# Sixteen gate tiles of a merge move into the state-space stage, and the order of dense steps and attention units changes

## The chip, the cores and the metric

The kernel runs on one core of a Trainium2 chip. A core has a matmul engine (TensorE), a vector engine (VectorE), an activation engine (ScalarE), a general one (GpSimd), and SyncE, which issues the DMAs here. The metric is the device time of one execution in microseconds. The kernel before takes 5170.65 us, the median of three runs (5169.60 to 5171.93).

## The reference

Everything is float32, with one sequence of 512 tokens (and 256 context tokens), model width 1024. A first block has two branches on a common projection `hl @ w_in`: RWKV, a recurrence over 16 heads, and a state-space model (SSM) over 4 groups of 8 heads with 128 states, chunk by chunk, in both directions, on the tokens in column-major order of a grid of 64 columns. The two are merged by gates, then come a router and 16 experts. The second block stands twice (two layers): dilated attention, latent attention and stick-breaking attention, three gated branches, and a feed-forward part. What the change touches:

```python
def merge(ya, yb, gates, p):
    ga, gb = jnp.split(jax.nn.sigmoid(gates.astype(F32)), 2, axis=-1)
    ya = jnp.einsum('blc,cd->bld', ya, p['proj_a'])
    yb = jnp.einsum('blc,cd->bld', yb, p['proj_b'])
    return jnp.einsum('bld,de->ble', ga * ya + gb * yb, p['w_out']).astype(gates.dtype)

# one chunk of the SSM (ssd_chunked), and stick-breaking attention of one block of 128 queries
y_intra = jnp.einsum('bijg,bijge,bjgep->bigep', cb, seg, xdt)
y_inter = jnp.einsum('bign,bgepn->bigep', c_c, h) * jnp.exp(cum)[..., None]
log_one_minus = jnp.where(strict, jax.nn.log_sigmoid(-z), 0.0)
after = lax.cumsum(log_one_minus, axis=3, reverse=True) - log_one_minus
weights = jnp.exp(jnp.where(strict, log_beta + after, -jnp.inf))
```

## The kernel before

The program has stages: start, RWKV, SSM, merge, experts, and twice the second block. Each stage has one function per engine (`ssm_sync`, `ssm_tensor`, `ssm_vector`, `ssm_scalar`, `ssm_gpsimd`, and so on), and between stages the engines meet: each waits until the other three have come (`meet`). Inside a stage a function yields the order of all steps, and each engine walks through this one order and issues its own share of every step, waiting on semaphores. TensorE thus works strictly in that order.

**SSM** (`ssm_order`, L1499). `turns` takes one step each from a list of generators in rotation: the decays, the forward scan, the projector, the backward scan, the projector again, the reader. So a turn has two projector steps. The projector makes, for each of four groups, six tiles `("conv", g, ci, s)` in seven steps (steps 0 to 3 hold two matmuls each of the projection, step 2 also the transposes of the tile before, steps 4 to 6 nothing for TensorE) and four tiles `("z", g, i, s)` of the gate z in two steps of four matmuls. A scanner has for each of six chunks `values`, `carry`, and for the four last ones also `masks`, `weights`, `apply`. `apply` multiplies the weights of the chunk with the values, eight heads of 64 columns in a bank of PSUM. The reader gates and squares the result (`read` 0 to 3) and transposes and stores it to DRAM (`ybd`, `read` 4 to 7). A group's projection starts when the read of the group two before is done (L1513), a group's scan when its z is done. The projections read `b.hp`, the input in column-major order; at the end of the stage `hp` is copied back to `k.hL` in row order, three engines at once, and the normalizer is brought to row order in `k.rb`.

**Merge** (`merge_tensor`, L2013). For each of eight tiles d of 128 output columns and each branch: eight matmuls with `hL` for the gate, then 8 (`proj_a`, on `yaT`) or 16 (`proj_b`, on `ybT`) for the branch. `yaT` (2 MB) and `ybT` (4 MB) are read from DRAM. SyncE loads weights into a ring of six areas, in the order `wg`, `pa`, `pb`.

**Second block** (`block2_order`, L2430). Attention units (head pair, block of 128 queries) run on six lanes. `drain` takes one step from each lane in rotation and mixes in dense steps (two matmuls of 512 columns, or four steps to a tile) of a second generator: each attention step adds n to `due`, and each whole unit of `due` takes one dense step. The stretches are: before meeting A (first projections and rotations), `softA` (dilated attention, with the latent projections), `softB` (latent attention), `stick` (stick-breaking) up to meeting C. The dense steps are the 24 gate tiles (`("gate", d, br, s)`, d from 0 to 7), `chan` and `tok`. A unit with row block i has 128(i + 1) keys, and in `Unit` (L2546) the units of `stick` take i = 0, 1, 2, 3 by pairs.

The helper lines that the rows name are L224 (a matmul), L227 (a transpose), L235 to L259 (VectorE), L282 (ScalarE), L337 (a load of a ring) and L470 (another load).

## Time and profile before

| | |
|---|---|
| median of three runs | 5170.65 us |
| profiled execution, own time | 5169.21 us |
| its span | 5167.4 us |
| TensorE busy | 4649.1 us (90%), 35892 instructions |
| VectorE, ScalarE, GpSimd busy | 2123.6, 1300.3, 435.4 us |
| mean clock of TensorE | 0.944 of full |
| DMA | 494.88 MB, mean 96 GB/s |

The span is from the first to the last instruction. A busy time counts an engine's instructions on that stretch; a matmul instruction of the program in float32 stands in the trace as two records. "Idle before" is the time in which an engine had nothing to do just ahead of the instruction, with what released it.

### The profile page before, as it was taken

Reading aid. Unit: us, or ns where it says so; the run is one execution under the profiler, and the core shown is the slowest. Engines: PE = TensorE matmul, PEld = TensorE weight load, DVE = VectorE, ACT = ScalarE, POOL = GpSimd, SP = SyncE. Lnnn points to the kernel's source line nnn. Section 1 sums busy time; section 2 is a strip of 40 time slices with the busy share of each in tenths; the row PEclk is TensorE's granted clock in tenths of the full one; section 3 lists DMA queues with packets and bytes.
Section 4 is the critical chain, followed back from the end, with each engine's and each line's share of the span. In section 5 each row is a group of like instructions: output and inputs, shape, how many; then the busy total and the mean of one; then the engine's idle time right before and its main releaser. Section 6 shows DMA issues by size and latency. Waiting matters only on the chain.

```text
span 5167.4 us, 84303 instructions
## 1 busy us (share of the span) xinstructions
PE 4649.1 (90%) x35892; PEld 2888.0 (56%) x35892; DVE 2123.6 (41%) x3933; ACT 1300.3 (25%) x2411; POOL 435.4 (8%) x387
## 2 busy tenths in 40 slices
PE   6899889988988969979999898979999998979999
PEld 3566666676554544465343554534777554544777
DVE  3555555553354461021111346473343346473333
ACT  2343333342222310010000123232232123241222
POOL 0121111110231330000000000020000000020000
PEclk8999999998989989989999899999999999989999
DMA  5200000001101004227999221113321221113221
GB/s 224 78 18 18 18 9 14 5 5 45 43 33 41 25 17 187 83 85 317 399 406 374 95 74 65 41 41 128 114 82 49 86 76 62 43 58 134 91 98 49
DMA packets 72783, 494.88 MB, mean 96 GB/s; under 512 B 9032, under 2 KB 9560, under 8 KB 29784
## 3 DMA queue, kind: packets, MB, share of 16 engines
q1 hardware_dynamic: 72408, 489.49, 24.5%
q8 instruction: 283, 4.64, 0.4%
q14 instruction: 92, 0.75, 0.0%
HBM read 468.47 MB, written 21.00 MB: 95 GB/s over the span
## 4 chain that ended last, share of the span: by engine, by line
PE 72%; issue 9%; DVE 9%; PEld 3%; DMA 3%; ACT 2%; POOL 1%; SPq 0%; PEldq 0%; POOLq 0%; DVEq 0%; ACTq 0%
PE ps L224 69%; PEld ps L224 3%; PE ps L227 3%; DMA upper<-in_ew 2%; DVE upper L235 2%; ACT upper L282 1%; DVE upper L243 1%; DVE upper L259 1%; POOL upper L3350 1%; DVE lower L235 1%; DVE upper L251 1%; DVE lower L243 1%; ACT lower L282 0%; DVE upper L239 0%; DVE lower L239 0%
## 5 line engine op out<-in xcount | busy, mean ns | idle before, releaser
L224 PE MATMUL ps<-lower 128*128 128x512 f32 (+9 forms) x6512 | 1967.3, 466 | 81.8 <-issue 25.1
L224 PEld LDWEIGHTS ps<-lower 128*128 128x128 f32 (+3 forms) x6512 | 997.4, 197 | 787.6 <-issue 609.4
L224 PE MATMUL ps<-upper 64*64 64x64 f32 (+7 forms) x15552 | 827.5, 258 | 125.4 <-DVE upper L251 44.0
L282 ACT ACTIVATE upper<-ps 128x512 f32<-128x512 f32 (+6 forms) x963 | 435.8, 483 | 1860.1 <-PE ps L224 1342.5
L224 PEld LDWEIGHTS ps<-upper 64*64 64x64 f32 (+4 forms) x15552 | 597.7, 145 | 437.2 <-issue 231.8
L224 PE MATMUL ps<-lower,upper 64*64 64x64 f32 (+6 forms) x7536 | 723.8, 315 | 55.2 <-DMA lower<-in_ada 20.8
L224 PE MATMUL ps<-rounded 128*128 128x512 f32 x3072 | 720.0, 397 | 30.6 <-DVE rounded L235 23.1
L224 PEld LDWEIGHTS ps<-rounded 128*128 128x128 f32 x3072 | 583.9, 190 | 165.9 <-ACT rounded L282 26.3
L224 PEld LDWEIGHTS ps<-lower,upper 64*64 64x64 f32 (+3 forms) x7536 | 383.0, 144 | 338.5 <-issue 279.7
L282 ACT ACTIVATE upper<-upper 128x768 f32<-128x768 f32 (+11 forms) x619 | 326.9, 534 | 735.8 <-DVE upper L255 205.8
L224 PE MATMUL ps<-upper,lower 128*128 128x512 f32 (+5 forms) x1584 | 483.0, 474 | 9.0 <-DVE lower L243 2.7
L259 DVE COPY_PREDICATED upper<-lower,ps 128x256 f32<-128x256 uint8 (+2 forms) x576 | 246.4, 457 | 326.5 <-PE ps L224 290.9
L224 PEld LDWEIGHTS ps<-upper,lower 128*128 128x128 f32 (+1 forms) x1584 | 249.3, 199 | 228.9 <-issue 211.4
L251 DVE COPY upper<-ps 128x64 f32<-128x64 f32 (+8 forms) x423 | 166.9, 405 | 449.6 <-PE ps L224 406.5
L227 PE MATMUL ps<-lower,upper 128*128 128x128 f32 (+1 forms) x1204 | 191.8, 294 | 132.0 <-ACT upper L282 61.4
L235 DVE TENSOR_TENSOR rounded<-lower,rounded 128x512 fp32r<-128x512 f32 (+2 forms) x136 | 200.9, 1477 | 257.4 <-ACT rounded L282 257.2
L235 DVE TENSOR_TENSOR upper<-upper,ps 128x512 f32<-128x512 f32 (+1 forms) x136 | 108.5, 798 | 481.6 <-PE ps L224 472.4
L282 ACT ACTIVATE rounded<-lower 128x512 fp32r<-128x512 f32 (+2 forms) x136 | 171.7, 1263 | 405.3 <-PE ps L224 270.3
L227 PEld LDWEIGHTS ps<-lower,upper 128*128 128x128 f32 (+1 forms) x1204 | 145.9, 148 | 223.2 <-issue 115.7
L282 ACT ACTIVATE lower<-ps 128x512 f32<-128x512 f32 (+1 forms) x178 | 104.5, 591 | 446.5 <-PE ps L224 416.7
L243 DVE SCALAR_TENSOR_TENSOR upper<-ps,lower,upper 128x511 f32<-128x511 f32 (+1 forms) x208 | 130.1, 625 | 141.0 <-ACT upper L282 135.1
L3337 POOL COPY upper<-lower 128x512 f32<-128x512 f32 x8 | 4.9, 613 | 2048.2 <-PE ps L224 2047.4
(81 smaller groups left out, 2193.2 us busy)
## 6 DMA issues: line engine op xcount, KB each, us to landing
lower<-in_ew SPq DMA_DIRECT2D x144, 1024.0 KB, 10.4
upper<-in_ew SPq DMA_DIRECT2D x48, 1024.0 KB, 13.5
lower<-in_b0f SPq DMA_DIRECT2D x16, 2048.0 KB, 7.8
lower<-in_b1f SPq DMA_DIRECT2D x16, 2048.0 KB, 7.7
upper<-in_ada SPq DMA_DIRECT2D x18, 1024.0 KB, 5.6
lower<-in_wrkv SPq DMA_DIRECT2D x8, 1728.0 KB, 7.6
lower<-in_b0g SPq DMA_DIRECT2D x8, 1536.0 KB, 6.4
gad<-upper SPq DMA_DIRECT2D x48, 256.0 KB, 2.0
```

Source lines behind the costliest of these rows:

```text
L224: return self.e.matmul(out, lhsT, rhs, start=start, stop=stop)
L227: return self.e.transpose(out, in_, self.ident[0:n, 0:n])
L235: self.e.tensor_tensor(out, a, b, op).then_inc(line.up(*event), 1)
L243: self.e.scalar_tensor_tensor(out, a, s, b, op0, op1).then_inc(line.up(*event), 1)
L251: self.e.tensor_copy(out, a).then_inc(line.up(*event), 1)
L259: self.e.copy_predicated(out, mask, data).then_inc(line.up(*event), 1)
L282: self.e.activation(out, in_, func, bias=bias, scale=scale, accum_out=accum).then_inc(line.up(*event), 1)
L3337: g.e.tensor_copy(b3[:, :, 0:64], v3(b.kv[:, i, :], 128)[:, :, 0:64]).then_inc(tail.pool.up(), 1)
L3350: g.e.tensor_tensor(y, y, r, SUB).then_inc(o.lane.pool.up("less", *o.u), 1)
```

## The change

The sixteen gate tiles of the merge are now steps of the SSM's projector (`mgate`, four steps of two matmuls to a tile), behind the last z tile. They read `hp`, ScalarE copies each tile to row order in one of two staging buffers, SyncE stores it to DRAM (`gmd`) and the merge reads it back before the sigmoid. `wg` is laid out in four blocks of 2 MB and runs through the SSM's ring of two areas. The copies of `hp` back to `hL` and the meeting ahead of them are gone. A group's projection starts when both scans of the group two before are done; its second tile waits until that group is gated. A group's scan starts before its z. The first two loads of the SSM are issued in the RWKV stage. `apply` has two matmuls of 64 stationary columns for one of 128.

In the second block the dense steps are counted by rounds of the lanes, one gate tile row (d = 4) moves behind the dense steps of `softB`, and the units of `stick` go from the long rows to the short ones.

```diff
@@ -827,6 +828,9 @@
     for name, j, *at in b.order:
         if name == "lora" and at == [1, 1] and j < 6:
             ring.load(("wrkv", j + 2), T["wrkv"][j + 2], P.pe, "lora", j + 2, 1, 1)
+        elif name == "lora" and at == [1, 1] and j == 7:
+            sp.wait_ge(P.pe, "lora", 7, 1, 1)
+            ssm_begin(k, sp)
         elif name == "ada_row" and j < 11:
@@ -1510,15 +1515,20 @@
 
     def projector():
         for g in range(4):
-            while g > 1 and g - 2 not in done:
+            while g > 1 and not {(g - 2, 0), (g - 2, 1)} <= scanned:
                 yield None
             for ci in range(6):
+                while g > 1 and ci and g - 2 not in gated:
+                    yield None
                 for s in range(7):
                     yield ("conv", g, ci, s)
+            ready.add(g)
             for i in range(4):
                 for s in range(2):
                     yield ("z", g, i, s)
-            ready.add(g)
+        for t in range(16):
+            for s in range(4):
+                yield ("mgate", t, s)
 
     def scanner(d):
         for g in range(4):
@@ -1538,6 +1548,8 @@
                 yield None
             for i in range(8):
                 yield ("read", g, i)
+                if i == 3:
+                    gated.add(g)
             done.add(g)
 
     proj = projector()
@@ -1555,26 +1567,37 @@
...
-def ssm_sync(k, sp):
...
-    ring.load(*next(loads))
-    ring.load(*next(loads))
+    loads += [(("wg", m), T["wg"][m], P.pe, "mgate", 4 * m + 3) for m in range(4)]
+    k.loads = iter(loads)
+    k.ring.load(*next(k.loads))
+    k.ring.load(*next(k.loads))
+
+
+def ssm_sync(k, sp):
+    b, T, P = k.ss, k.T, k.proj
+    for e in k.end:
+        sp.wait_ge(k.end[e], "rwkv")
...
+            sp.wait_ge(P.act, "mgate", t)
+            sp.e.dma_start(k.gmd[t], b.stage[t % 2]).then_inc(k.kept[t % 2].up16("gate", t), 16)
+        if name == "dt" or name == "conv" and z[1:] in ([3, 3], [5, 3]) or name == "z" and z[1:] == [3, 1] or (
+                name == "mgate" and z[0] % 4 == 3 and z[1] == 3):
+            load = next(k.loads, None)
             if load:
-                ring.load(*load)
...
+    def merge_gate(t, s):
+
+        use = ("mgate", t)
+        w, loaded = k.slot["wg", t // 4]
+        w = v3(w, 512)
+        if s == 0:
+            at["mgate"] = pb.take(use)
+            pe.wait_ge(loaded, "wg", t // 4)
+        for kk in (2 * s, 2 * s + 1):
+            last = pe.mm(at["mgate"], ch(w[:, kk, :], t % 4), b.hp[:, kk, :], kk == 0, kk == 7)
+        if s == 3:
             last.then_inc(P.pe.up(*use), 1)
             pb.give(use, P.act, *use)
 
...
                 v = slice(64 * x, 64 * x + 64)
-                last = pe.mm(p2[:, v], ch(b.Wt[d], x), b.xd[d][:, v], True, True)
+                for e in (slice(0, 64), slice(64, 128)):
+                    last = pe.mm(p2[e, v], ch(b.Wt[d], x)[:, e], b.xd[d][:, v], True, True)
             last.then_inc(team.pe.up("apply", g, i), 1)
             banks.give(use2, team.dve, "new", g, i)
...
     last.then_inc(M.pe.up("yrstd"), 1)
-    pe.meet("pe", "scan")
     pe.meet("pe", "ssm")
 
...
-    v.meet("dve", "scan")
-    for kk in (1, 4, 7):
-        v.copy(M.dve, k.hL[:, kk, :].rearrange("p (r c) -> p r c", c=64), b.hp[:, kk, :].rearrange("p (c r) -> p r c", r=8))
+    v.wait_ge(M.pe, "yrstd")
     v.copy(M.dve, k.rb.rearrange("p (r c) -> p c r", c=64), k.pair("yrstd").rearrange("p (c r) -> p c r", r=8))
     v.meet("dve", "ssm")
...
-        elif s == 2 and ci:
+        if s == 2 and ci:
+            if ci == 1 and g > 1:
+                a.wait_ge(tail.dve, "gated", g - 2, 3)
             turn(g, ci - 1)
...
+        elif name == "mgate":
+            t, s = z
+            if s == 3:
+                a.wait_ge(P.pe, "mgate", t)
+                if t > 1:
+                    a.wait_ge(k.kept[t % 2], "gate", t - 2)
+                a.copy(P.act, b.stage[t % 2].rearrange("p (r c) -> p c r", c=64),
+                       k.pair(("mgate", t)).rearrange("p (c r) -> p c r", r=8), "mgate", t)
...
     a.act(M.act, s4, s4, AF.Exp, "yrstd", scale=-0.5)
-    a.meet("act", "scan")
-    for kk in (0, 3, 6):
-        a.copy(M.act, k.hL[:, kk, :].rearrange("p (r c) -> p r c", c=64), b.hp[:, kk, :].rearrange("p (c r) -> p r c", r=8))
     a.meet("act", "ssm")
...
-    load("wg", 0)
+    def gates(d):
+        if d > 1:
+            sp.wait_ge(M.dve, "mT", d - 2)
+        for br in range(2):
+            sp.e.dma_start(b.sig[br][d % 2], k.gmd[2 * d + br]).then_inc(k.line(f"gate_in{d % 2}_{br}").up16("gate", d), 16)
+
     load("pa", 0)
     for line in k.stored:
...
     fetch(sp, b.ybT, k.ybd.rearrange("k p t -> p k t"), "ybT")
-    for name in ("wg", "pa", "pb"):
+    gates(0)
+    for name in ("pa", "pb"):
         load(name, 1)
+    gates(1)
...
         for br, (name, src, nk, source) in enumerate((("pa", b.yaT, 8, "yaT"), ("pb", b.ybT, 16, "ybT"))):
-            ps = banks.take(("gate", d, br))
-            pe.wait_ge(loaded_g, "wg", d)
-            for kk in range(8):
-                last = pe.mm(ps, wg[:, kk, 128 * br:128 * br + 128], k.hL[:, kk, :], kk == 0, kk == 7)
-            last.then_inc(M.pe.up("gate", d, br), 1)
-            banks.give(("gate", d, br), M.act, "gate", d, br)
             w, loaded = k.slot[name, d]
...
-            if d > 1:
-                a.wait_ge(M.dve, "mT", d - 2)
-            a.act(M.act, b.sig[br][d % 2], k.pair(("gate", d, br)), AF.Sigmoid, "gate", d, br)
+            a.wait_ge(k.line(f"gate_in{d % 2}_{br}"), "gate", d)
+            a.act(M.act, b.sig[br][d % 2], b.sig[br][d % 2], AF.Sigmoid, "gate", d, br)
     for i in range(4):
...
             ready.add(name)
-        yield from gates(range(5))
+        yield from gates(range(4))
 
     def half(par):
@@ -2504,40 +2543,42 @@
             yield None
         yield from tok("c2")
         ready.add("c")
-        yield from gates(range(5, 8))
+        yield from gates(range(4, 8))
 
     def drain(gens, other, n):
 
         gens, due = list(gens), 0.0
         while gens:
-            for z, g in enumerate(list(gens)):
+            turn = list(gens)
+            for z, g in enumerate(turn):
                 step = next(g, 0)
                 if step == 0:
                     gens.remove(g)
                 elif step is not None:
                     out.append(step)
-                    due += n
-                while due >= 1 and z % 2:
+                if z % 2 or len(turn) == 1:
+                    due += n / max(len(turn) // 2, 1)
+                while due >= 1:
                     out.append(next(other, None))
                     due -= 1
 
     out += tok("a0")
     out += tok("a1")
     filler = dense()
-    drain([half(0), half(1)], filler, 2)
+    drain([half(0), half(1)], filler, 4)
     while "lat" not in ready:
         out.append(next(filler))
     out.append(("meet", "A"))
-    drain([lane("softA", 48, 4, z) for z in range(6)] + [latent(), latent_rope(0), latent_rope(1)], filler, 0.25)
+    drain([lane("softA", 48, 4, z) for z in range(6)] + [latent(), latent_rope(0), latent_rope(1)], filler, 1.2)
     out += filler
     out.append(("meet", "latent"))
     out += [("bT", s, z) for s in range(2) for z in range(8)]
     filler = dense_c()
-    drain([lane("softB", 32, 4, z) for z in range(6)] + [mixture()], filler, 0.4)
+    drain([lane("softB", 32, 4, z) for z in range(6)] + [mixture()], filler, 1.8)
     while "c" not in ready:
         out.append(next(filler))
     out.append(("meet", "B"))
-    drain([lane("stick", 32, 5, z) for z in range(6)], filler, 0.25)
+    drain([lane("stick", 32, 5, z) for z in range(6)], filler, 1.4)
     out += filler
     out.append(("meet", "C"))
     return [s for s in out if s is not None]
@@ -2550,6 +2591,8 @@
         b, c2 = k.b2[l], k.c2
         self.u, self.lane, self.buf = (name, l, u), k.lane[u % 6], b.lanes[u % 6]
         hh, i = 2 * (u // 8) + u % 2, u // 2 % 4
+        if name == "stick":
+            hh, i = 2 * (u // 2 % 4) + u % 2, 3 - u // 8
         e = slice(64 * (hh % 2), 64 * (hh % 2) + 64)
         self.i, self.n0, self.nk, self.q = i, 0, 128 * (i + 1), 4 * hh + i
         if name == "softA":
```

In the last group's scan, TensorE's order was this. `128x512` from `lower,upper` is the state product (`apply` first, then `carry`), `128x64` the application of the weights, `128x128` the decays.

```order
4702 L224 MATMUL ps<-lower,upper 128x512 [waits step0_dve]
4703 L224 MATMUL ps<-lower 128x64 [waits step1_pool,step1_dve,step0_act]
4704 L224 MATMUL ps<-lower 128x64 x7
4705 L224 MATMUL ps<-lower,upper 128x512 [waits step1_act]
4706 L224 MATMUL ps<-lower 128x64 [waits step0_pool,step0_dve,step0_act]
4707 L224 MATMUL ps<-lower 128x64 x7
4708 L224 MATMUL ps<-lower,upper 128x512 [waits step1_dve] x2
4709 L224 MATMUL ps<-upper 128x128 [waits step0_dve]
4710 L224 MATMUL ps<-lower 128x128 [waits step1_pool,step0_dve]
```

Now the same place, where `128x512` from `lower` are gate matmuls and `64x64` the application in halves:

```order
4734 L224 MATMUL ps<-lower,upper 128x512 [waits step0_dve]
4735 L224 MATMUL ps<-lower 64x64 [waits step1_pool,step1_dve,step0_act]
4736 L224 MATMUL ps<-lower 64x64 x15
4737 L224 MATMUL ps<-lower 128x512 x2
4738 L224 MATMUL ps<-lower,upper 128x512 [waits step1_act]
4739 L224 MATMUL ps<-lower 64x64 [waits step0_pool,step0_dve,step0_act]
4740 L224 MATMUL ps<-lower 64x64 x15
4741 L224 MATMUL ps<-lower 128x512 [waits proj_act]
4742 L224 MATMUL ps<-lower 128x512
4743 L224 MATMUL ps<-lower,upper 128x512 [waits step1_dve]
4744 L224 MATMUL ps<-lower 128x512 x2
```

Two gate matmuls stand between any two steps of the scan that were neighbours. At the change from one stage to the other TensorE's order was this, from the normalizer's matmuls on:

```order
4731 L227 MATMUL ps<-lower,upper 128x128 [waits tail_dve]
4732 L227 MATMUL ps<-lower,upper 128x128 x3
4733 L224 MATMUL ps<-lower 128x128 [waits main_dve,step1_dve]
4734 L224 MATMUL ps<-lower 128x128 x3
4735 L224 MATMUL ps<-lower 128x512 [waits end_act,end_pool,end_dve,end_pe,weights0]
4736 L224 MATMUL ps<-lower 128x512 x7
4737 L224 MATMUL ps<-upper,lower 128x512 [waits yaT,weights1]
4738 L224 MATMUL ps<-upper,lower 128x512 x7
4739 L224 MATMUL ps<-lower 128x512 x8
```

and is now this, with the last gate tile at its head:

```order
4789 L227 MATMUL ps<-lower,upper 128x128 x4
4790 L224 MATMUL ps<-lower 128x512 x4
4791 L224 MATMUL ps<-lower 128x512 [waits proj_act]
4792 L224 MATMUL ps<-lower 128x512 x7
4793 L224 MATMUL ps<-lower 128x128 [waits main_dve,step1_dve]
4794 L224 MATMUL ps<-lower 128x128 x3
4795 L224 MATMUL ps<-upper,lower 128x512 [waits end_pool,weights0,end_act,yaT,end_dve,end_pe]
4796 L224 MATMUL ps<-upper,lower 128x512 x7
4797 L224 MATMUL ps<-upper,lower 128x512 [waits ybT,weights1]
4798 L224 MATMUL ps<-upper,lower 128x512 x15
```

The merge's first matmul now waits for `yaT` too, and the gate matmuls ahead of the two branches are gone. SyncE's row has the following at that place, `ybd` being stores of the last two groups:

```order
46 L1581 DMA ybd<-upper 128x512 [waits tail_dve] x8
47 L337 DMA lower<-in_wg 128x2048 [waits end_act,end_pool,end_dve,end_pe]
48 L337 DMA lower<-in_pa 128x1024
49 L470 DMA upper<-yad 128x8x512 [waits stored1,stored0]
50 L337 DMA lower<-in_pb 128x2048
```

and now, `gmd` being stores of gate tiles:

```order
56 L1595 DMA gmd<-upper 128x512 [waits proj_act] x4
57 L337 DMA lower<-in_wg 128x4096 [waits proj_pe]
58 L1595 DMA gmd<-upper 128x512 [waits proj_act] x5
59 L1604 DMA ybd<-upper 128x512 [waits tail_dve] x2
60 L1595 DMA gmd<-upper 128x512 [waits proj_act]
61 L1604 DMA ybd<-upper 128x512 [waits tail_dve] x2
62 L1595 DMA gmd<-upper 128x512 [waits proj_act] x2
63 L337 DMA lower<-in_pa 128x1024 [waits end_act,end_pool,end_dve,end_pe]
```

Thirteen gate stores are ahead of the last group's first `ybd` and three behind. The end of stick-breaking in the first layer was this on TensorE (`64x64` a value product, L227 the transposes):

```order
5900 L227 MATMUL ps<-lower,upper 128x128 [waits lane0_act]
5901 L227 MATMUL ps<-lower,upper 128x128 x3
5902 L227 MATMUL ps<-lower,upper 128x128 [waits lane1_act]
5903 L227 MATMUL ps<-lower,upper 128x128 x3
5904 L224 MATMUL ps<-upper 64x64 [waits lane4_act,lane2_dve]
5905 L224 MATMUL ps<-upper 64x64 x5
5906 L224 MATMUL ps<-upper 64x64 [waits lane5_act,lane3_dve]
5907 L224 MATMUL ps<-upper 64x64 x5
5908 L224 MATMUL ps<-upper 64x64 [waits lane0_dve]
```

and is now this:

```order
5908 L224 MATMUL ps<-lower 128x512 [waits proj_dve]
5909 L224 MATMUL ps<-lower 128x512
5910 L224 MATMUL ps<-upper 64x64 [waits lane0_act]
5911 L224 MATMUL ps<-upper 64x64
5912 L224 MATMUL ps<-upper 64x64 [waits lane1_act]
5913 L224 MATMUL ps<-upper 64x64
5914 L224 MATMUL ps<-lower 128x512 x6
5915 L224 MATMUL ps<-lower 128x512 [waits proj_dve]
5916 L224 MATMUL ps<-lower 128x512 x7
```

Eight dense matmuls of one tile and six of another, the last of the block, stand where the last units stood.

## Rows read from the trace of the kernel before

**Rows 1.** Part 1 of the page: engine, busy us (share), instructions.

```profile
PE 4649.1 (90%) x35892; PEld 2888.0 (56%) x35892; DVE 2123.6 (41%) x3933; ACT 1300.3 (25%) x2411; POOL 435.4 (8%) x387
```

**Rows 2.** Table by stretches, state-space stage and merge: length, engines' busy us, clock, DMA.

```profile
1343.00:1489.00 146.00, 134.55 (x559) 85.52 (x558) 69.27 (x101) 41.00 (x50) 43.75 (x32) 0.96 0.08 29
1489.00:1516.00 27.00, 16.27 (x79) 11.94 (x77) 24.18 (x23) 6.53 (x14) 20.04 (x12) 0.75 0.19 69
1516.00:1680.00 164.00, 140.83 (x533) 85.87 (x532) 71.48 (x105) 34.91 (x47) 26.25 (x20) 0.91 0.09 34
1680.00:1834.00 154.00, 142.54 (x582) 89.84 (x581) 69.37 (x102) 42.05 (x51) 43.80 (x33) 0.97 0.06 21
1834.00:1912.00 78.00, 56.72 (x316) 42.92 (x315) 60.92 (x65) 13.26 (x25) 44.92 (x28) 0.87 0.04 14
1912.00:1945.00 33.00, 7.35 (x32) 5.37 (x31) 19.80 (x29) 6.69 (x13) 2.94 (x2) 0.55 0.19 70
1945.00:2222.00 277.00, 276.63 (x640) 122.58 (x640) 23.16 (x32) 10.84 (x17) 0.00 (x0) 0.99 0.32 123
```

**Rows 3.** Chain of waits, the merge's piece: start, us, what.

```profile
1945.37 276.94 PE ps L224 x640
```

**Rows 4.** Timeline, end of the stage: start, us, instructions, idle before <- releaser.

```profile
1841.79 1.19 PE L224 MATMUL ps<-lower,upper 128*128 128x512 f32 x1 [4.10 <-POOL lower L1949]
...
1933.66 2.05 PE L224 MATMUL ps<-lower 128*128 128x128 f32 x8 [3.26 <-DVE lower L239]
...
1939.35 1.02 DVE L251 COPY lower<-ps 128x512 f32<-128x512 f32 x1
1940.48 0.33 SPq L337 DMA_DIRECT2D lower<-in_wg  x1
```

**Rows 5.** Timeline of TensorE: one application of weights, then one value matmul.

```profile
1608.26 1.89 PE L224 MATMUL ps<-lower 128*128 128x64 f32 x16
1609.99 1.08 PE L224 MATMUL ps<-lower,upper 128*128 128x512 f32 x2
...
3434.15 1.15 PE L224 MATMUL ps<-upper 128*64 128x64 f32 x32
3435.23 3.70 PE L224 MATMUL ps<-lower 128*128 128x512 f32 x8
```

**Rows 6.** DMA issues at the merge's start: count, KB each, us to landing.

```profile
upper<-ybd SPq DMA_DIRECT2D x1, 4096.0 KB, 22.6
...
upper<-yad SPq DMA_DIRECT2D x1, 2048.0 KB, 11.5
```

**Rows 7.** Table by stretches, attention of the first layer; last row second layer.

```profile
3029.00:3211.00 182.00, 176.32 (x932) 85.61 (x930) 100.91 (x283) 64.98 (x194) 4.69 (x8) 0.99 0.19 70
3232.00:3364.00 132.00, 131.88 (x676) 68.50 (x676) 54.86 (x168) 36.08 (x104) 0.00 (x0) 1.00 0.11 43
3364.00:3461.00 97.00, 85.40 (x452) 40.04 (x448) 72.05 (x141) 37.82 (x90) 22.95 (x25) 0.96 0.12 43
3461.00:3493.00 32.00, 14.34 (x144) 10.17 (x144) 25.34 (x44) 11.78 (x25) 8.86 (x9) 0.68 0.09 29
4515.00:4612.00 97.00, 85.32 (x444) 39.98 (x444) 72.39 (x139) 37.77 (x90) 23.78 (x25) 0.96 0.12 43
```

**Rows 8.** VectorE by forms, stick-breaking: busy us, mean ns, then idle before.

```profile
L2984 DVE TENSOR_TENSOR_SCAN upper<-upper 128x512 f32<-128x512 f32 x8 | 14.9, 1865 | 0.3
L243 DVE SCALAR_TENSOR_TENSOR upper<-upper 128x512 f32<-128x512 f32 x16 | 11.2, 699 | 0.3
...
L251 DVE COPY upper<-ps 128x512 f32<-128x512 f32 x13 | 8.6, 679 | 8.0 <-PE ps L227 6.3 <-PE ps L224 1.7
...
L2984 DVE TENSOR_TENSOR_SCAN upper<-upper 128x128 f32<-128x128 f32 x8 | 5.1, 632 | 0.3
L243 DVE SCALAR_TENSOR_TENSOR upper<-upper 128x128 f32<-128x128 f32 x16 | 4.5, 282 | 0.6 <-ACT upper L282 0.3
```

**Rows 9.** Timeline of TensorE: eight matmuls of 512 columns after a wait.

```profile
1646.54 10.07 PE L224 MATMUL ps<-lower 128*128 128x512 f32 x16 [1.27 <-DVE upper L239]
```

46 lines of the change are left out of this document (23 added, 23 removed).

## Prediction

> **What bounds the kernel now.** The page's first part comes first: TensorE is busy for 90% of the span and has nine times as many instructions as any other engine [rows 1]. So the question is where its idle tenth lies, and whether the change puts work there. The second view is the busy time by stretches of the two stages that the change joins [rows 2]. The reader is to see two kinds of stretch. From 1343 to 1834 the projections and the scans of the state-space stage run together; TensorE idles 11.4, 10.7, 23.2 and 11.5 us in the four stretches, 56.8 us together. From 1834 on no projection is left, and the last group's scan is a relay between engines: 56.7 us of work in 78 us, then 7.4 us in 33. The merge that follows is the opposite, 276.6 busy of 277, and the chain of waits has it as one piece of 640 matmul records [rows 3]: there every microsecond of matmuls taken out is a microsecond of span. Third, the last steps in order of time [rows 4]: in the tail TensorE waits up to 4.1 us for GpSimd, and after the normalizer's matmul (1933.66) come the copies back into hL and the last copy before SyncE may issue the merge's loads at 1940.5; I call that moment S. Fourth, the same table for the attention of the first layer [rows 7]: the softmax stretches 3029 to 3211 and 3232 to 3364 are full (176.3 of 182, 131.9 of 132), the stick-breaking one isn't: 11.6 of 97 and 17.7 of 32 us idle. The second layer repeats it.
>
> **Prices.** 276.94 us over 640 records are 0.433 us for a record of 512 columns [rows 3]; a matmul has two. A gate tile (8 matmuls, 16 records) is 6.92 us, all sixteen 110.8 us. A dense step of the attention (2 matmuls) is 1.73 us.
>
> **The change, part by part.**
> Gates into the tail. The 64 steps now come two per turn behind the last projection, with the group-3 scan between them. The stretch from 1834 to 1912 holds its own 56.7 us of TensorE work and 110.8 more. Each turn gives 3.5 us of matmuls that need nothing of the scan, and a wait of the scan such as the 4.1 us before 1841.79 [rows 4] has a turn or two of gates ahead of it; so I take 4 us of idle as left: 171.5 us in place of 78, **+93.5**. Ends of the guess: 0 idle, or the present 21.3.
> The end of the stage. From 1912 to S pass 28.5 us: VectorE's last read, the transposes, the normalizer, copies. The read and the variance now lie beside gate matmuls (six steps, 10.4 us, are behind the last transpose); the copy of eight slices back into hL is gone. Left are the normalizer's matmul, 2.05, VectorE's copy, 1.02, and 0.6 for the meeting [rows 4]: 3.7, **-24.8**. The copies and stores of the gate tiles are on ScalarE (13.3 us busy of 78 there, so there is room for sixteen copies) and SyncE. Three tiles' stores stand in SyncE's queue behind the last group's; they can delay the tile two later by the two staging buffers, some 2 us, within my 4.
> The middle. A group's projection now starts when the scan two before is done, not its read. That fills 1489 to 1516, which has no projection: 10.7 idle, and the clock is at 0.75 there, so about 4 us of slow matmuls. 1516 to 1680 should fall from 23.2 idle to the 11.5 of the stretches around it, 12. Together **-27**; ends -10 (waits only move) and -40.
> Applying the weights: 8 matmuls with 128 stationary columns become 16 with 64, in alternate halves. Now 16 records take 1.73 us from start to next start [rows 5]. The attention's value matmuls have the new shape: 32 records in 1.08 us [rows 5]. 0.65 us for each of 32 applications is 20.8; most of them are where TensorE is full, so **-19**; ends -21 and 0.
> The Trainium skill, "TensorE: Matmul & The Clock Gate", section on LDWEIGHTS, says that a load costs by its columns, about P/1.2 ns. For 128 columns that is 107 ns, and the trace agrees (1.73 us over 16 is 108). For 64 it is 53 ns, so by this rule alone 32 loads cost the same 1.7 us and the sum would be 19 higher; the row of the value matmuls, 34 ns a record, says that loads in alternate halves overlap, and the row decides. The skill's "TensorEngine Tiling (Array Packing)", Key Properties, adds that a change of tiling mode drains the engine; the 1.08 us holds that already.
> The earlier weight loads at the start of the stage: 0, since TensorE starts there at VectorE's copies into hp, and the first projection is behind the dt matmuls.
> So S moves by 93.5 - 24.8 - 27 - 19 = **+22.7**.
> The merge. Before, 1940.5 to 2222.3 is 281.8. Now nothing covers the first loads. yaT lands 11.5 us after its issue with 3.5 MB up to and with it, ybT 22.6 after its own, 25.7 after S, with 8.5 [rows 6]; a megabyte less each gives 9.3 and 23 after S. First branch product 6.9 plus 2.3 for a cold clock, then the wait to 23, 13.8 for the second, then seven times 24 matmuls, 20.8: 23 + 13.8 + 145.4 = 182.2. **-99.6**. The sixteen tiles read back are 4 MB in 180 us, two per 20.8 us, and bind nothing. State-space stage and merge: **-77**.
> Attention, each layer. By the order of the program 7 gate steps move ahead of the first meeting (1 to 8), the first softmax loses 19 (59 to 40), the second 4 (53 to 49), and stick-breaking gains 16 (31 to 47). Ahead: +12.1, TensorE is full there. First softmax: -32.9, of which 4 come back since VectorE (100.9 of 182 busy) is late more often: -28.9. Second: -6.9. Stick-breaking: 99.7 us of TensorE work in 129 us becomes 127.4. VectorE's work stays at 97.4, so TensorE is the longer now, but the long rows come first: a unit of 512 keys costs VectorE three passes of 0.70, a scan of 1.87 and a copy of 0.68, 4.6 us, one of 128 keys three of 0.28 and 0.63, 1.5 [rows 8]. On TensorE the 32 units cost 99.7 less 31 dense steps, 46 us; shared out by keys that is 2.3 us for the longest and 0.6 for the shortest. A round of six lanes has 1.2 units and 1.4 dense steps: 5.6 us on VectorE and 5.2 on TensorE in the long quarter, 1.8 and 3.1 in the short one. So stalls stay in the first third, some 13 us, and the present empty tail of 17.7 is gone: 140, **+11**. Layer: -12.7; two layers **-25**. Ends: stick-breaking 0 or all 27.7.
> Sum: -77 - 25 = -102 against the profiled execution's own 5169.2, so 5067; the median of the runs is 1.4 above that execution: **5068 us**.
>
> **Rivals.**
> *Stick-breaking doesn't take the 16 steps in.* For it: 72.1 of 97 us of VectorE in the first part, and the long rows together. Against it: the tail's idle. Then +27.7 in place of +11, twice: 5068 + 33 = 5101.
> *The SSM's middle stays as it is and the halves don't overlap.* For it: the idle time there is made of chains, not of missing work (conv steps 4 to 6 have no matmul). +17 + 19: 5104. The skill's rule on LDWEIGHTS is its half of 19 us.
> *It goes better:* no idle left in the tail (-4), the middle -40 (-13), the halves in full (-2), stick-breaking no longer than before (-22): 5027.
> *Gate tiles are held up by their way out* (bank, copy, staging, store in SyncE's row behind a read): 2 us for each of 16, 5100.
> *Slower: the clock in the tail.* 1834 to 1912 has a mean clock of 0.87, and eight matmuls of 512 columns after a wait took 10.07 us [rows 9] where sixteen records at full clock are 6.92. If the scan's waits held the clock at the lower of its two levels (1.2 GHz) through the tail, the gates would cost 110.8 us more and the scan's products some 28: 5068 + 139 = 5207. It decides once all sixteen tiles run so (110.8 against a gain of 102). Against it: with projections between the scan's steps the rows show 0.96 and 0.97 [rows 2], and gates are like those.
>
> **How the numbers follow.** Forecast 0.58 (own range 5040 to 5095), stick-breaking 0.15, middle and halves 0.12, better 0.10, way out 0.02, clock 0.03. The range that leaves out no more than 2 in 10: half of the better case below, the rivals at 5101 to 5104 inside: 5035 to 5112. A measurement tells 0.2%, 10 us, from nothing. Slower is the clock case, 0.03; within 0.2% needs several rivals at once, 0.02; faster 0.95.
>
> **What will show it.** Right: the stretch from the last projection to S with TensorE above 95% and clock near 1; S 15 to 30 us later; the merge's branch part near 180 us with 384 records and one wait for ybT; 32 records of an application in 1.1 us; stick-breaking at 135 to 145 us, ending on dense matmuls. Wrong: idle of 20 us or more left in the tail, gate matmuls waiting for ScalarE, a merge that waits for gate tiles, or stick-breaking beyond 150 us with VectorE full in its first half.

## The result and the profile after

The changed kernel takes 5123.86 us (median of four runs, 5119.18 to 5129.86), the kernel before 5171.29 in the same comparison: a ratio of 0.9907 (0.9890 to 0.9924), about 48 us less. I had said 5068, 102 less, and a range up to 5112. The profiled execution spans 5126.6 us, 40.8 less than that of before. TensorE's part of the page, against [rows 1]:

```profile
PE 4632.3 (90%) x36404; PEld 2855.7 (56%) x36404; DVE 2122.7 (41%) x3930; ACT 1307.9 (26%) x2422; POOL 431.9 (8%) x385
```

Its busy time fell by only 17 us, and its share of the span is still 90%, so the profile's totals say nothing of where the missing time went. The tables by stretches do.

**State-space stage and merge.** The table by stretches answers to [rows 2] (length, then busy us of PE, PE's loads, VectorE, ScalarE, GpSimd, clock, DMA share, GB/s). The first gate tile's store is issued at 1813.5.

```profile
1343.00:1800.00 457.00, 413.64 (x2130) 248.46 (x2129) 245.33 (x334) 122.89 (x162) 134.13 (x94) 0.95 0.10 37
1800.00:1909.00 109.00, 106.45 (x569) 58.84 (x567) 45.59 (x53) 21.50 (x29) 31.70 (x21) 1.00 0.24 90
1909.00:1945.00 36.00, 34.19 (x117) 15.84 (x116) 12.56 (x17) 7.71 (x13) 0.00 (x0) 1.00 0.12 44
1945.00:1969.50 24.50, 18.26 (x45) 8.63 (x44) 4.51 (x9) 2.27 (x4) 0.00 (x0) 0.87 0.15 54
1993.00:2153.00 160.00, 159.86 (x368) 70.43 (x368) 23.16 (x32) 11.35 (x17) 0.00 (x0) 0.99 0.40 149
```

The first stretch still idles 43 us of 457; the second, where gates stand between the scan's steps, 2.6 of 109, at clock 1.00. That part came out as forecast, and the clock rival fell. The end of the stage and the start of the merge in the chain of waits answer to [rows 3, 4]:

```profile
1966.36 1.96 PE ps L224 x8
...
1968.34 1.02 DVE lower L251
...
1969.47 0.33 SPq L337
...
1970.96 22.04 DMA upper<-ybd
...
1993.14 159.88 PE ps L224 x368
```

The moment S (SyncE may issue the merge's loads) is 1969.5, 29 us later than 1940.5 (forecast 22.7). The last matmul of the branches ends at 2153.0, 183.5 after S (forecast 182.2), with one wait for the read of `ybT`, 22 us. Up to there 69.3 us are gained; up to the second block's norm 71.2.

**Attention.** Answers to [rows 7], first layer: first softmax, second, the first two thirds of stick-breaking, the rest.

```profile
2970.00:3137.00 167.00, 147.91 (x854) 73.76 (x854) 98.64 (x280) 63.05 (x194) 4.69 (x8) 0.96 0.17 60
3159.20:3290.50 131.30, 127.63 (x660) 66.28 (x660) 54.82 (x169) 35.68 (x105) 0.22 (x1) 0.99 0.09 31
3290.50:3387.00 96.50, 82.95 (x482) 41.41 (x483) 78.53 (x123) 37.79 (x74) 24.51 (x21) 0.93 0.17 63
3387.00:3431.00 44.00, 41.32 (x172) 18.69 (x170) 21.26 (x62) 12.66 (x42) 6.72 (x12) 1.00 0.13 46
```

Here the forecast fails. The first softmax has 19 dense steps fewer, 32.9 us of work, in a stretch only 14.6 us shorter: 19.1 us idle of 167 at clock 0.96, where it was 5.7 of 182 at 0.99. The view of TensorE's waits (us in total, times, longest) says that it waits longer for VectorE's L243. The first softmax before, then changed:

```profile
PE ps L224 <- DVE upper L243: 1.8, 3, 0.9
```

```profile
PE ps L224 <- DVE upper L243: 13.1, 11, 4.2
```

The table has the stage lengths of the first layer for all kernels, worked out from starts in TensorE's timeline (each stage's first matmul of its own form; the last column ends with the piece of 160 records that follows stick-breaking in the chain of waits). Dense steps are given as ahead of the first meeting (gate steps only, behind 112 others in every kernel), first softmax, second, stick-breaking. "Three" is the sum of the three attention stages, "rest" the untouched part up to the next layer's norm.

| kernel | steps | ahead | both softmax | stick | three | rest |
|---|---|---|---|---|---|---|
| before | 1/59/53/31 | 160.2 | 336.0 | 133.6 | 469.6 | 509.6 |
| changed | 8/40/49/47 | 172.3 | 320.7 | 145.8 | 466.5 | 514.2 |
| 1 state-space part only | 1/59/53/31 | 159.3 | 335.2 | 133.6 | 468.8 | 509.7 |
| 2 second block only | 8/40/49/47 | 172.1 | 320.5 | 145.7 | 466.2 | 514.3 |
| 5 gates back behind the meeting | 1/47/49/47 | 160.1 | 322.2 | 145.5 | 467.7 | 508.9 |
| 6 new rule, counts of before | 1/59/53/31 | 158.9 | 337.7 | 144.2 | 481.8 | 509.6 |
| 7 as 6, long rows first | 1/59/53/31 | 158.7 | 337.7 | 146.0 | 483.7 | 508.6 |
| 8 changed, old unit order | 8/40/49/47 | 171.7 | 316.4 | 152.7 | 469.1 | 514.3 |
| 11 as 5, stick pace 1.7 | 1/47/49/47 | 161.7 | 321.5 | 144.7 | 466.1 | 512.0 |
| 12 as 11, latent pace 2.2 | 1/47/55/41 | 161.8 | 328.3 | 137.2 | 465.6 | 513.2 |

The changed kernel's account over before is then: -71.2 up to the second block; first layer +12.1 ahead of the meeting, -15.3 in both softmax stages, +12.2 in stick-breaking, +4.6 in the rest; the second layer +14.0, -13.9, +12.3, and +4.2 at the end. Together -40.9, the 40.8 of the two spans.

### The profile page after: what moved, and what is told of

The parts are those of the page before. It is cut to its first block, busy times and chain, and to the rows that moved or that the text cites. A ratio compares the mean times of both kernels' runs of the same rounds, so it can differ in the third digit from the quotient of the medians.

```text
span 5126.6 us, 85359 instructions
## 1 busy us (share of the span) xinstructions
PE 4632.3 (90%) x36404; PEld 2855.7 (56%) x36404; DVE 2122.7 (41%) x3930; ACT 1307.9 (26%) x2422; POOL 431.9 (8%) x385
## 4 chain that ended last, share of the span: by engine, by line
PE 78%; DVE 8%; issue 6%; DMA 3%; ACT 2%; POOL 1%; SPq 0%; PEldq 0%; PEld 0%; DVEq 0%; ACTq 0%; POOLq 0%
PE ps L224 75%; PE ps L227 3%; DMA upper<-in_ew 2%; DVE upper L243 2%; ACT upper L282 2%; DVE upper L259 1%; DVE upper L235 1%; POOL upper L3393 1%; DVE lower L235 1%; DVE upper L251 1%; DVE lower L243 1%; ACT lower L282 1%; DMA upper<-ybd 0%; DVE upper L239 0%; DVE lower L239 0%
## 5 line engine op out<-in xcount | busy, mean ns | idle before, releaser
L224 PE MATMUL ps<-lower 128*128 128x512 f32 (+12 forms) x7024 | 1940.7, 445 | 66.0 <-issue 22.8
L224 PEld LDWEIGHTS ps<-lower 128*128 128x128 f32 (+3 forms) x7024 | 960.3, 188 | 782.2 <-issue 610.4
L282 ACT ACTIVATE upper<-ps 128x512 f32<-128x512 f32 (+5 forms) x967 | 444.8, 491 | 1783.7 <-PE ps L224 1297.2
L282 ACT ACTIVATE upper<-upper 128x768 f32<-128x768 f32 (+10 forms) x631 | 333.7, 536 | 763.2 <-DVE upper L255 202.5
L224 PE MATMUL ps<-upper,lower 128*128 128x512 f32 (+4 forms) x1584 | 480.8, 473 | 25.5 <-DMA upper<-yad 11.5
L251 DVE COPY upper<-ps 128x64 f32<-128x64 f32 (+9 forms) x423 | 167.0, 405 | 462.8 <-PE ps L224 429.8
L282 ACT ACTIVATE rounded<-lower 128x512 fp32r<-128x512 f32 (+2 forms) x136 | 171.7, 1263 | 414.1 <-PE ps L224 279.1
L227 PE MATMUL ps<-lower,upper 128*128 128x128 f32 (+1 forms) x1204 | 188.3, 290 | 85.8 <-ACT upper L282 42.6
L227 PEld LDWEIGHTS ps<-lower,upper 128*128 128x128 f32 (+1 forms) x1204 | 146.3, 147 | 180.4 <-issue 73.3
L282 ACT ACTIVATE lower<-ps 128x512 f32<-128x512 f32 (+1 forms) x174 | 102.2, 592 | 391.6 <-PE ps L224 362.2
L243 DVE SCALAR_TENSOR_TENSOR upper<-ps,lower,upper 128x511 f32<-128x511 f32 (+1 forms) x208 | 130.1, 625 | 133.6 <-ACT upper L282 127.9
```

The lines of the kernel that those rows point to most:

```text
L224: return self.e.matmul(out, lhsT, rhs, start=start, stop=stop)
L227: return self.e.transpose(out, in_, self.ident[0:n, 0:n])
L243: self.e.scalar_tensor_tensor(out, a, s, b, op0, op1).then_inc(line.up(*event), 1)
L251: self.e.tensor_copy(out, a).then_inc(line.up(*event), 1)
L282: self.e.activation(out, in_, func, bias=bias, scale=scale, accum_out=accum).then_inc(line.up(*event), 1)
```

## Experiments

Each was timed in three rounds beside the kernel before, whose median on the chips used was 5172 to 5177, so ratios are compared, not times.

**1. Only the state-space part.** The second block as before (all four edits of its order undone):

```diff
-    drain([half(0), half(1)], filler, 4)
+    drain([half(0), half(1)], filler, 2)
...
-        if name == "stick":
-            hh, i = 2 * (u // 2 % 4) + u % 2, 3 - u // 8
```

> The changed kernel with the second block's order of the kernel before (dense steps, gate block and stick-breaking units as they were). Theory 1: the state-space and merge part brought its 71 us (as the first norm after the experts stood 71.2 us earlier in the changed kernel's trace) and the second block gave 30 of them back. Then 5171 - 71 = 5100, some 25 to 30 us under the changed kernel, and each layer takes 1151 us again. Rival, the prediction's own size: the state-space part is worth 77 and the attention part only lost what the execution's clock lost: 5094. Rival 2, the second block's loss is not from its order but from the clock of a program that is shifted in time: then it stays, and the kernel takes about 5124 as the changed one does.

Measured 5099.5, ratio 0.9852 (0.9837 to 0.9866), 77 us under before and 24 under the changed kernel (by the medians 5099.5 and 5123.9). Each layer is back at its old lengths. Theory 1 holds (5100, and 25 to 30 under the changed kernel), and the interval holds the prediction's 77 for this part as well as the trace's 71.

**2. Only the second block's part**, on the kernel before.

```diff
-        yield from gates(range(5))
+        yield from gates(range(4))
...
-    drain([half(0), half(1)], filler, 2)
+    drain([half(0), half(1)], filler, 4)
```

> The kernel before with only the second block's changes (rounds, one gate block moved, long rows first). Theory 1: the attention stages cost 9 us more in each layer, as in the changed kernel (+12 ahead of the first meeting, -15 in the first softmax, -1 in the second, +12 in stick-breaking): 5171 + 18 = 5189, or up to 5200 if the 6 us a layer that the feed-forward part lost there belong to the change too. Rival, the prediction: -25, so 5146. Rival 2, the loss is a shift in time of the clock: 5171.

Measured 5200.5, ratio 1.0046 (1.0031 to 1.0061): slower by 24 us, the upper end of theory 1. In the first layer its stage lengths are those of the changed kernel within 0.2 us, the 5 us of the rest too (514.3; 523.6 at the end where before has 518.8). So the loss is this part's own and no accident of where in time it stands.

**3 and 9. The weights in halves**, alone on the kernel before (3), and undone in the changed one (9, shown):

```diff
-                for e in (slice(0, 64), slice(64, 128)):
-                    last = pe.mm(p2[e, v], ch(b.Wt[d], x)[:, e], b.xd[d][:, v], True, True)
+                last = pe.mm(p2[:, v], ch(b.Wt[d], x), b.xd[d][:, v], True, True)
```

> The kernel before with only the weights applied in halves of 64 columns. The prediction: -19 us, 5152. Theory now: the busy time of this form fell from 68.3 to 39.3 us in the state-space stage, but the wait ahead of it (22.8 us by the trace, 25.1 before) did not; if the order of the kernel before is bound by such chains, a part of the 29 us turns into waits and -15 to -25 stay, 5146 to 5156. Rival, the rule that a load costs by its columns (107 ns for 128, 53 for 64): 0, 5171, and 32 records would take 1.7 us.

> The changed kernel with the weights applied by whole tiles of 128 columns as before. Theory 1: in the changed order TensorE is full in the last group's scan, so there the whole 0.65 us or more of an application counts, and the form's busy time (39.3 us against 68.3) is the price: +18 to +29, so 5142 to 5153. Rival, it is worth what it was in the kernel before (14 us), since chains bind elsewhere: 5138. Rival 2, the prediction's 19: 5143.

3 measured 5163.5, ratio 0.9973 (0.9962 to 0.9983), -14 us; 9 measured 5146.6, ratio 0.9938 (0.9921 to 0.9956), +16 against the changed kernel's ratio. The chain of waits gives it more sharply, as the distance from the first long piece of the state-space stage to the output projection of the merge. Before:

```profile
1211.93 43.27 PE ps L224 x176
...
2224.04 55.51 PE ps L224 x256
```

1012.1 us. With halves only:

```profile
1220.00 43.32 PE ps L224 x176
...
2218.47 55.51 PE ps L224 x256
```

998.5, so -13.6. Changed, and changed with whole columns:

```profile
1212.65 42.89 PE ps L224 x176
...
2154.72 55.51 PE ps L224 x256
```

```profile
1218.86 43.18 PE ps L224 x176
...
2178.61 55.51 PE ps L224 x256
```

942.1 and 959.8, so 17.7. The forecast was 19. How sure such a difference is, other executions tell: in the three traces whose state-space part is the old one (before, 2, 4) the distance is 1010.5 to 1015.0, and in the eight that have the changed one (changed, 1, 5, 6, 7, 8, 11, 12) it is 942.1 to 943.2 in seven and 937.7 in one. So about 5 us either way is possible. An application in the changed kernel's timeline, against [rows 5]:

```profile
1850.98 3.06 PE L224 MATMUL ps<-lower 128*64 128x64 f32 x36
1853.88 1.02 PE L224 MATMUL ps<-lower,upper 128*128 128x512 f32 x2
```

The first row joins 32 records of the application with 4 of a gate step, 2.90 us from start to start; 4 records at 0.433 are 1.73, so 1.17 us are left (37 ns a record) where 16 whole ones took 1.73. By forms, before and after (busy us, mean ns, idle ahead):

```profile
L224 PE MATMUL ps<-lower 128*128 128x64 f32 x512 | 68.3, 292 | 25.1 <-issue 25.1
```

```profile
L224 PE MATMUL ps<-lower 128*64 128x64 f32 x1024 | 39.3, 233 | 22.8 <-issue 22.8
```

29 us of busy time are gone, the waits ahead of the form are not, and 14 to 18 us reach the stage. The Trainium skill's rule that a load costs by its columns ("TensorE: Matmul & The Clock Gate", LDWEIGHTS) would have made 3 and 9 zero; these traces disagree for loads in alternate halves (37 ns a record, not 53).

**10. Wait for the read again.**

```diff
-            while g > 1 and not {(g - 2, 0), (g - 2, 1)} <= scanned:
+            while g > 1 and g - 2 not in done:
```

> The changed kernel where a group's projection waits again for the read of the group two before, not only for its scans. The prediction gave the new condition 27 us (10 to 40). Theory 1, from the traces: TensorE's idle between 1343 and the last projection only fell from 56.8 to 45.9 us, so about 10 us: 5134. Rival, the prediction's size: 5151. Rival 2, the waits only move: 5124.

Measured 5138.3, ratio 0.9934 (0.9913 to 0.9954): +14 by the two ratios, with an uncertainty as large. The same distance in the chain of waits tells more:

```profile
1211.18 42.76 PE ps L224 x176
...
2160.35 55.51 PE ps L224 x256
```

949.2 us, 7.1 more than the changed kernel and 6 to 11.5 more than the eight traces above. So the condition is worth some 7 us, about what theory 1 had and at the prediction's lower bound of 10; its 27 is refuted. Most of the idle time in the middle was not the work of this condition. That a group's scan now starts before its z, and the earlier first loads, were not tried by themselves.

**4 and 8. The order of the stick-breaking units**, alone on the kernel before (4), and undone in the changed one (8, shown).

```diff
-        if name == "stick":
-            hh, i = 2 * (u // 2 % 4) + u % 2, 3 - u // 8
```

> The kernel before with only the units of stick-breaking from long to short rows; 31 dense steps there, as before. Theory: the empty tail of 17.7 us with its 6.5 us wait shrinks to some 5 while the first third gets fuller waits: stick-breaking goes from 128 us to 118 to 124, so 4 to 10 us a layer less, 5151 to 5163. Rival: VectorE is the bound of the long rows (5.6 us a round against TensorE's 4.6), so that what the tail gives back is lost in the first third: 0, 5171. Rival 2: slower, by up to 6 us a layer, 5183.

> The changed kernel with the stick-breaking units in their old order (47 dense steps as in the changed one). Theory 1, the order is worth nothing: 5124, stick-breaking 146 us. Rival, the prediction's: the 16 added steps were taken in for 12 us only because the long rows come first; without it 5 to 10 us a layer more, 5134 to 5144. Rival 2: the old order mixes long and short units and is better under this load, 2 to 5 us a layer less.

4: 5170.6, ratio 0.9992 (0.9982 to 1.0002), nothing, so its main theory falls. The first rival has the right number, but not the right reason, as the windows show. 8: 5150.0, ratio 0.9950 (0.9931 to 0.9969), 22 us over the changed kernel's ratio. The stick-breaking stage by one window each, in the kernel before and in 4:

```profile
3364.80:3498.40 133.60, 104.10 (x629) 54.51 (x629) 100.30 (x186) 52.64 (x121) 31.80 (x33) 0.90 0.14 50
```

```profile
3365.00:3498.70 133.70, 108.61 (x628) 56.35 (x629) 101.24 (x186) 52.38 (x120) 31.43 (x33) 0.89 0.15 56
```

TensorE's idle falls from 29.5 to 25.1 us, but its busy time for the same matmuls rises by 4.5, at clock 0.89 for 0.90: nothing is left. The waits were not lost again in the first third, as that rival had it; the same matmuls took longer. In the changed kernel and in 8:

```profile
3290.50:3436.40 145.90, 128.87 (x693) 64.51 (x693) 103.25 (x189) 53.51 (x122) 31.23 (x33) 0.95 0.18 66
```

```profile
3286.30:3439.00 152.70, 131.83 (x692) 65.18 (x693) 102.41 (x189) 53.48 (x122) 31.54 (x33) 0.94 0.17 62
```

With 47 dense steps the order is worth 6.8 us a layer, 3.8 of waits and 3.0 of busy time. The prediction's rival for 8 (5 to 10 us a layer) was right on the stage: with the old order it is longer. (The rest of the 22 to 26 us between the medians isn't in these stages; the profiled execution of 8 spans 5136.2, and its four runs lie between 5138 and 5158.)

**6 and 7. Only the rule by rounds**, with as many dense steps in each stretch as before, and the same with long rows first:

```diff
-    drain([half(0), half(1)], filler, 4)
+    drain([half(0), half(1)], filler, 3)
...
-latent_rope(1)], filler, 1.2)
+latent_rope(1)], filler, 1.75)
...
-    drain([lane("stick", 32, 5, z) for z in range(6)], filler, 1.4)
+    drain([lane("stick", 32, 5, z) for z in range(6)], filler, 0.9)
```

> The changed kernel with the gate block where it was, the stick-breaking units in their old order, and the rounds' numbers chosen so that each stretch holds as many dense steps as before (113, 59, 53 and 31); only the rule that spreads them is new. Theory 1, the number of steps in a stretch is what counts: as the kernel with only the state-space part, 5100, with 133.6 us for stick-breaking. Rival, even spreading is better by itself, since the last part of stick-breaking gets dense steps too: 5085 to 5092. Rival 2, the rule is worse by itself (steps come where no lane waits) and made part of the loss: 5110 or more.

> The same (113, 59, 53, 31 dense steps, new rule) with the stick-breaking units from long to short rows as in the changed kernel. Theory 1, the long rows first leave as much waiting in the first third as they take from the end (their order alone took the same 133.7 us in the kernel before): the same as with the old order under this rule, within 3 us a layer. Rival, order and even spreading help only together: 5 to 8 us a layer less, 5085 to 5090.

6 measured 5121.8, ratio 0.9894 (0.9879 to 0.9909); 7 5126.8, ratio 0.9912 (0.9892 to 0.9933). Theory 1, that only the number of steps counts, falls, and rival 2 of 6 (the rule is worse by itself, 5110 or more) holds: 6 is 22 us slower than 1 with the same numbers. The stick-breaking stage in 1, 6 and 7:

```profile
3303.30:3436.80 133.50, 104.47 (x628) 54.54 (x629) 100.30 (x186) 52.54 (x120) 31.77 (x33) 0.90 0.14 49
```

```profile
3294.80:3439.00 144.20, 113.82 (x629) 57.25 (x629) 100.92 (x186) 53.03 (x121) 31.52 (x33) 0.85 0.11 39
```

```profile
3298.40:3444.40 146.00, 110.57 (x629) 55.47 (x629) 100.83 (x186) 52.57 (x121) 31.15 (x33) 0.88 0.11 39
```

1 and 6 execute the same matmuls (628 and 629 records in the windows) and idle nearly the same, 29.0 and 30.4 us. 6 is 10.7 us longer, and 9.3 of that is that the same matmuls take 113.8 us instead of 104.5, at a mean clock of 0.85 against 0.90. In 1 the 31 steps stand in the first five sixths (six among 24 attention steps); in 6 they are spread thinly (three to five among 24) and the last eight stand at the end. In stretches of 10 us the clock is under 0.9 in 5 of 13 in kernel 1, the lowest of them in its empty tail, and in 8 of 14 in kernel 6, all along. Three stretches of 1 and three of 6:

```profile
3393.00:3403.00 10.00, 7.36 (x47) 3.55 (x46) 8.98 (x13) 3.03 (x9) 3.80 (x4) 1.00 0.01 5
3403.00:3413.00 10.00, 6.24 (x68) 4.22 (x68) 7.75 (x19) 3.34 (x9) 1.54 (x2) 0.83 0.27 88
3413.00:3423.00 10.00, 1.80 (x8) 1.00 (x6) 9.79 (x15) 4.79 (x9) 3.35 (x3) 0.54 0.00 1
```

```profile
3355.00:3365.00 10.00, 9.08 (x51) 4.72 (x52) 6.42 (x18) 4.41 (x12) 1.27 (x4) 0.69 0.01 2
3385.00:3395.00 10.00, 6.17 (x18) 2.65 (x15) 7.89 (x12) 4.03 (x10) 3.79 (x4) 0.67 0.12 48
3405.00:3415.00 10.00, 5.36 (x19) 2.54 (x20) 9.79 (x15) 5.29 (x10) 2.82 (x3) 0.70 0.02 6
```

One with 0.9 us of waits has a clock of 0.69: in 6 it stays low after waits elsewhere. With the steps close together it falls less, but for the tail (0.54 and 0.61 in its last two stretches). In 7, against 4, the idle time rises as well (35.4 us for 25.1): fewer of its 31 steps stand beside the long rows (12 among the first 72 attention steps, where 4 has 17), which would explain it but was not tried by itself.

The six kernels set side by side show what the stick-breaking stage of the first layer (us) owes to the rule, to the number of steps and to the order of the units:

| rule, dense steps | old order | long rows first |
|---|---|---|
| old rule, 31 | 133.6 (1) | 133.7 (4) |
| by rounds, 31 | 144.2 (6) | 146.0 (7) |
| by rounds, 47 | 152.7 (8) | 145.8 (changed) |

The rule alone costs 10.6 or 12.3 us. Under it, the 16 added steps, 27.7 us of work, cost 8.5 us in the old order and nothing with the long rows first: TensorE's idle time falls from 35.4 to 17.0 us, and the clock is 0.95 for 0.88. So the changed kernel's +12.2 is the price of the rule and not that of the steps. The old rule with 47 steps was not tried.

**5, 11 and 12. Where the steps stand.** 5 puts the seven steps ahead of the meeting back into the first softmax:

```diff
-    drain([half(0), half(1)], filler, 4)
+    drain([half(0), half(1)], filler, 3)
...
-latent_rope(1)], filler, 1.2)
+latent_rope(1)], filler, 1.4)
```

> The changed kernel with the rounds' numbers 3 and 1.4 in place of 4 and 1.2 in the first two stretches: the seven gate steps that had moved ahead of the first meeting go back into the first softmax (47 dense steps there, not 40). Theory 1, from the changed kernel's stages (a step ahead of the meeting costs its full 1.73 us, one of the 19 taken from the first softmax gave back only 0.77): -12.1 + 5.4 a layer, so about 13 us faster than the changed kernel, 5110. Rival, seven steps fit into the 19 us of idle for nothing: -24, 5100. Rival 2, TensorE is bound there in the end, the steps cost what they cost: 0, 5124.

11 and 12 add to it another pace in stick-breaking, and 12 also one in the latent stage:

```diff
-[mixture()], filler, 1.8)
+[mixture()], filler, 2.2)
...
-    drain([lane("stick", 32, 5, z) for z in range(6)], filler, 1.4)
+    drain([lane("stick", 32, 5, z) for z in range(6)], filler, 1.7)
```

> The best so far (the first two stretches' numbers 3 and 1.4, 5093 us) with stick-breaking's number 1.7 in place of 1.4, so that its 47 dense steps come earlier, with the long rows, and four are left for the end in place of twelve. Theory 1, its waits and its low clock lie in the first half (4.8 and 2.5 us idle, clock 0.75 and 0.66 in two stretches of 10 us of the changed kernel) while the end is full: 3 to 6 us a layer less, 5081 to 5087. Rival, VectorE is the bound with the long rows, more dense steps there only delay it: 0 to +3 a layer, 5093 to 5099.

> As the one before, with the latent attention's number 2.2 in place of 1.8: 55 dense steps there (49 before) and 41 in stick-breaking. Theory 1: a dense step costs 1.73 us in the full latent stretch and gives back about 0.8 in stick-breaking, less the 4.4 us of waits and some low clock that the latent stretch has now: +6 - 5 a layer, so within 3 us a layer of the one before. Rival, the latent stretch then keeps its full clock as in the kernel before: 4 us a layer less. Rival 2, full price on one side and nothing back on the other: +10 a layer.

5 measured 5092.9, ratio 0.9841 (0.9826 to 0.9857), 31 us faster than the changed kernel by medians, 7 more than the rival's 24, which the two intervals allow. The window of its first softmax:

```profile
2951.40:3120.00 168.60, 157.01 (x884) 76.78 (x884) 99.53 (x282) 64.02 (x195) 4.05 (x8) 0.99 0.17 61
```

157.0 us of work in 168.6, where the changed kernel had 148 in 167: seven steps, 12.1 us of work, for 1.5 us over both softmax stages. That is within the spread of executions: over both layers the two stages take 316.4 to 322.9 us in the kernels with the changed kernel's steps (changed, 2, 8, 9, 10) and 319.1 to 322.2 in those with seven more (5, 11). The rival that they go in free is right; from 47 steps down the first softmax hardly gets shorter. No engine is full there (VectorE 99.5 of 168.6), and most of what TensorE waits for is VectorE's L243, so I take the units' own chain over the engines as what holds it; that was not tried by itself. Ahead of the meeting the steps had cost their full price, 12.2 us in the first layer and 12.4 in the second. That is 24.6 of the 39.8 us between the two profiled spans; nearly all of the rest lies in stages that 5 does not touch (6.2 up to the second block, 5.3 in the first layer's rest, 2.7 at the end) and is no effect of the edit that these runs could show.
11: 5096.9, 0.9845 (0.9829 to 0.9861). 12: 5094.1, 0.9842 (0.9827 to 0.9857). Neither differs from 5 measurably; theory 1 of 11 (3 to 6 us a layer less) falls, its stage won 0.8; for 12 it holds (within 3 us a layer). In 12, six steps moved cost 6.8 us in the softmax stages and gave back 7.5 in stick-breaking. 5, 11 and 12 beat both kernels of the case, by some 30 and 80 us.

## Why the prediction was wrong

**Direction and the merge: right.** The merge is the best term: 183.5 us against 182.2, with 368 records in one piece after the wait for `ybT`. The first branch's product took 8.97 us where I had 6.9 and 2.3 for the clock, and `ybT` was there 23.7 us after S (forecast 23). The tail with the gates in it is full at clock 1.00, so the clock rival did not come; of the one on the way out there are only 1.8 us, two waits of gate matmuls for ScalarE.

**S: a sum that came near through errors of both signs.** +29.0 against +22.7, of which 0.7 arose ahead of the stage. The middle brought 7.1 in place of 27 (experiment 10), the halves 17.7 in place of 19 (9). What is left, the gates and the end of the stage, is therefore 28.3 + 24.8 = 53.1 where I had 93.5 - 24.8 = 68.7. No experiment divides these 15.6 us. The stretch from 1343 to S, before and changed, shows where they may lie:

```profile
1343.00:1940.50 597.50, 498.26 (x2093) 321.46 (x2091) 315.00 (x422) 144.44 (x197) 181.71 (x126) 0.91 0.08 29
1343.00:1969.50 626.50, 572.55 (x2858) 331.78 (x2856) 308.00 (x412) 154.38 (x208) 165.83 (x114) 0.96 0.13 48
```

The idle time fell by 45.3 us, and the busy time rose by 74.3. Gates of 110.8 less the 29.0 of the halves would be 81.8; the 7.5 that are missing go with the mean clock, which rose from 0.91 to 0.96. Gate steps also start before the point where I let them start (the first gate store is issued at 1813.5, with most of the last group's scan still to come). One error goes the other way: the 7.4 us of matmuls between 1912 and 1945 are left out of the end of the stage but for 2.05, and are counted nowhere else. The failing step here was to take all idle time above the neighbours' as fillable by an earlier start.

**The attention: the step that failed** is "First softmax: -32.9, of which 4 come back since VectorE (100.9 of 182 busy) is late more often: -28.9". The reason was right and the size was not: 18 came back, and the stretch gave 14.6. I priced the removed steps by TensorE, because it was full (176.3 of 182 busy) and VectorE was not (100.9). But full only meant that 59 dense steps filled the units' waiting. From 112 to 96 steps in the two softmax stages under one rule (6 to 5) 27.7 us of work went and 15.5 us of time; the next seven, 12.1 us, brought 1.5. "Second: -6.9" is of the same kind: from the transposes ahead of it to stick-breaking, TensorE's busy time fell from 141.3 to 137.6, its idle time rose from 1.5 to 4.5, and 0.7 us was gained. The rest of each layer, 4 to 5 us more, I had at 0.

**The rule by rounds: a term that I put at nothing.** I counted how many dense steps each stretch has and gave no price to how they are spread. With the counts and the unit order of before, the rule costs 22 us (experiment 6 against 1): in the first layer 10.6 in stick-breaking and 2.5 in the two softmax stages. That alone is nearly the 24 us by which the second block's part slows the kernel. What the changed kernel adds to 6, the moved steps and the new order of the units, leaves its time where it was (5123.9 against 5121.8).

**Stick-breaking: the size was right by luck.** +11 forecast, +12.2 measured (experiment 2 has the same), with 17 us of waits in place of 29.5. I gave the 11 us to the 16 added steps; with the long rows first they cost nothing (146.0 us with 31 steps in 7, 145.8 with 47), and the 12.2 us are the rule's, 133.7 to 146.0 between 4 and 7. Of the reasons, "the long rows come first ... So stalls stay in the first third" held (13.6 us of idle up to 3387, 2.7 after), though it is ScalarE's L282 that releases most of these waits (15.0 us of 17) and not VectorE, and 8 shows that the order pays with the added steps. What I had not seen is that the mix matters through the clock.

**Ahead of the meeting: right** (+12.1 and 12.1), but I didn't ask what it buys. Experiment 5: nothing. Its rival would have been: seven steps of 1.73 us moved to a full stretch from one that cannot use their absence, 24 us over both layers. I had weighed what added steps cost in stick-breaking and not what removed steps leave in the softmax.

So 102 forecast against 41 in the two profiled executions: 6 are the state-space part (77 against 71), 47 the attention stages (-12.7 a layer forecast; +9.1 and +12.4 measured, without the rest), and 9 the rest of the layers. The likely rival, stick-breaking that takes nothing in, named the wrong stage; the range left out that a stage would refuse to shrink.

**What stays open.** Why the untouched rest of a layer takes 511 to 514 us in the first layer and 523 or 524 in the second in the kernels with the changed kernel's step counts (changed, 2, 8, 9, 10), and 509 or 510 and 517 to 519 in those with the counts of before, under either rule (before, 1, 3, 4, 6, 7); 5, 11 and 12 lie between, at 509 to 513 and 518 to 520. The trace shows only that the clock differs: after the same gap, between the same two pieces of the feed-forward part, in before and in the changed kernel:

```profile
3776.00:3796.00 20.00, 17.11 (x74) 13.64 (x73) 6.13 (x5) 5.06 (x4) 0.00 (x0) 1.00 0.28 106
```

```profile
3714.00:3734.00 20.00, 17.11 (x63) 13.41 (x62) 3.68 (x3) 4.58 (x4) 0.00 (x0) 0.83 0.29 106
```

17.11 us busy in both, but 74 records at clock 1.00 and 63 at 0.83. What decides it was not tried. Also open are the wait of 22.8 us ahead of the applications that the trace puts down to "issue", and what stick-breaking with 47 steps would take under the old rule.
